# New tables of moves for the second, third and fourth mixer of a four-mixer transformer kernel; the instructions stay the same

## What is computed

```python
def reference(x, ...):
    x = first_block(x, ...)     # layer 0: even_mixer, layer 1: odd_mixer
    return second_block(x, ...) # layer 0: even_mixer_2 + swiglu, layer 1: odd_mixer_2 + swiglu

def odd_mixer(h, w_in, w_out, ...):            # the second mixer, stage "odd"
    proj = h @ w_in
    hq, hf, hi, hg, lx, lg = split_cols(proj, ODD_SIZES)
    hc = rms_norm(hgrn2(hq, hf, hi, lb)) * silu(hg)
    hl = rg_lru(causal_conv(lx, conv_w, conv_b), ...) * silu(lg)
    return concat(hc, hl) @ w_out

# the third mixer, stage "diff": differential attention beside a 31-tap convolution
# the fourth mixer, stage "ssm": latent attention beside a complex state-space scan
```

## Time and profile before

| | us |
|---|---|
| median of 3 runs | 1750.78 (1749.95 to 1752.95) |
| the profiled execution, its own time | 1755.67 |
| its span from first to last instruction | 1753.9 |
| TensorE busy in the span | 1699.9 (97%) |
| VectorE, ScalarE, GpSimd busy | 961.7, 769.7, 949.0 |
| share of the chain that ended last | TensorE 81%, VectorE 11%, ScalarE 4% |

### The profile page before, as it was taken

One profiled execution on the slowest core, in us unless ns is written; L12 is line 12 of the kernel. 1 busy time (PEld: TensorE's weight loads), 2 busy tenths in 40 slices (PEclk: granted clock), 3 DMA queues, 4 the chain that ended last, 5 costly groups with the idle time before them and its releaser, 6 DMA issues.

```text
span 1753.9 us, 21148 instructions
## 1 busy us (share of the span) xinstructions
PE 1699.9 (97%) x7871; PEld 1324.0 (75%) x7871; DVE 961.7 (55%) x1504; ACT 769.7 (44%) x1314; POOL 949.0 (54%) x1108
## 2 busy tenths in 40 slices
PE   9999999998999999899999999999999999999997
PEld 6767668776878776687888888875457888888886
DVE  2033555779966898747614313369786752132344
ACT  4254675477475334754322222354335533222232
POOL 4433224678964463235656656569354565565662
PEclk9999999999999999899999999999999999999998
DMA  5221112222112221022322222221001222222221
GB/s 210 83 84 61 36 49 96 95 73 84 49 37 86 83 85 49 26 83 97 108 97 96 96 96 97 96 72 48 13 24 49 85 96 101 92 97 100 96 96 69
DMA packets 39702, 139.96 MB, mean 80 GB/s; under 512 B 4528, under 2 KB 4656, under 8 KB 39472
## 3 DMA queue, kind: packets, MB, share of 16 engines
q1 hardware_dynamic: 39600, 138.61, 23.4%
HBM read 136.50 MB, written 2.10 MB: 79 GB/s over the span
## 4 chain that ended last, share of the span: by engine, by line
PE 81%; DVE 11%; ACT 4%; issue 2%; POOL 1%; DMA 0%; SPq 0%; DVEq 0%; ACTq 0%
PE ps L889 19%; PE ps L891 18%; PE ps L890 18%; PE ps L910 1%; PE ps L960 1%; PE ps L917 1%; PE ps L962 1%; PE ps L961 1%; DVE ps L1101 1%; PE ps L1178 1%; PE ps L1176 1%; PE ps L1177 1%; PE ps L906 1%; PE ps L1312 1%; PE ps L1636 1%
## 5 line engine op out<-in xcount | busy, mean ns | idle before, releaser
L3165 POOL TENSOR_TENSOR wl<-raw,wh 128x256 fp32r<-128x256 f32 x988 | 801.3, 842 | 710.0 <-ACT wh L1034 704.0
L1034 ACT ACTIVATE wh<-raw 128x1024 fp32r<-128x1024 f32 x246 | 259.4, 1056 | 479.9 <-PE ps L891 441.0
L889 PE MATMUL ps<-hh,wh 128*128 128x512 f32 x1028 | 414.6, 403 | 2.4 <-ACT arena L1472 0.8
L891 PE MATMUL ps<-hh,wl 128*128 128x512 f32 x1028 | 401.3, 390 | 0.0
L890 PE MATMUL ps<-hl,wh 128*128 128x512 f32 x1028 | 401.0, 390 | 0.0
L889 PEld LDWEIGHTS ps<-hh,wh 128*128 128x128 f32 x1028 | 193.5, 188 | 56.2 <-issue 12.0
L890 PEld LDWEIGHTS ps<-hl,wh 128*128 128x128 f32 x1028 | 193.5, 188 | 42.8 <-issue 4.5
L891 PEld LDWEIGHTS ps<-hh,wl 128*128 128x128 f32 x1028 | 193.4, 188 | 41.0
L889 PE MATMUL ps<-mh,wh 128*128 128x512 f32 x540 | 220.0, 407 | 3.4 <-DVE ml L2955 1.4
L891 PE MATMUL ps<-mh,wl 128*128 128x512 f32 x540 | 211.2, 391 | 0.0
L890 PE MATMUL ps<-ml,wh 128*128 128x512 f32 x540 | 210.9, 391 | 0.0
(11 more groups left out here) (497 smaller groups left out, 2746.7 us busy)
## 6 DMA issues: line engine op xcount, KB each, us to landing
raw<-in_w SPq DMA_DIRECT2D x246, 512.0 KB, 3.3
x<-in_x SPq DMA_DIRECT2D x8, 256.0 KB, 8.3
out<-x SPq DMA_DIRECT2D x8, 256.0 KB, 2.0
arena<-in_rope SPq DMA_DIRECT2D x3, 512.0 KB, 4.7
arena<-in_dec SPq DMA_DIRECT2D x1, 1024.0 KB, 6.3
mats<-in_mats SPq DMA_DIRECT2D x1, 576.0 KB, 9.4
raw<-in_w SPq DMA_DIRECT2D x2, 256.0 KB, 3.7
arena<-in_lw SPq DMA_DIRECT2D x1, 512.0 KB, 4.1
```

What stands on the lines that cost most here:

```text
L889: e.matmul(ps[b][:], a, xh, start=first, stop=False)
L891: e.matmul(ps[b][:], l, xh, start=False, stop=final).then_inc(pe.sem, pe.up(*step))
L1034: e.activation(wh[:, n % NHL, :], raw[:, n % NRAW, :], ACT.Copy).then_inc(rounded.sem, rounded.up(n))
L3165: e.tensor_tensor(wl[:, n % NHL, cut(i, 2)], raw[:, n % NRAW, cut(i, 2)], wh[:, n % NHL, cut(i, 2)].bitcast(F32), SUB).then_inc(split.sem, ...
```

## The change

The tables `AHEAD["odd"]`, `AHEAD["diff"]` and `AHEAD["ssm"]` are replaced: 158, 214 and 146 moves become 184, 243 and 164. The table of `even`, the functions that write the first order, the instructions and the order of the weight stream are the same; every engine issues the same instructions in another order. What the new tables were laid out with is an estimate in which a VectorE operation on two tiles in SBUF lasts longer beside a GpSimd operation; that estimate is not in the kernel. In the file the second mixer's table begins so:

```diff
     "odd": [
-        (('w', ('p', 6), 3), ('hn3', 2)), (('hn4', 1), ('w', ('p', 6), 2)), (('hn4', 0), ('hn4', 1)), (('hn3', 1), ('w', ('p', 6),
...
```

## The result

The changed kernel takes **1733.99 us** (median of 4, 1733.88 to 1735.5) against 1751.61 for the kernel before in the same comparison: a ratio of 0.9902, 95% interval 0.9885 to 0.9919. That is 17.2 us less by the ratio and 17.6 by the medians. The forecast was 1743.5 with a range of 1737 to 1754: the direction was right, the gain more than twice the forecast and outside the range. The two profiled executions lie 20.2 us apart (1755.67 and 1735.5), so their stages show some 3 us more than the medians.

The account below looks back on a forecast made before the run. It took TensorE's 34.4 us of idle time in three mixers plus the low clock as the bound, VectorE and GpSimd setting the pace in 380:490. Terms -5.3 + 0 - 2.0 = -7.3 from 1750.8 gave 1743.5 us, range 1737 to 1754.

Parts of the forecast that it names:

- the 0 for the third mixer: Third mixer: new and covered waits taken to leave the stage unchanged, 0 us (-3 to +2.4).
- the -2.0 for the fourth: Fourth mixer: VectorE's two-tile operations run shorter while GpSimd idles; -2.0 us, part of the clock included (-5 to +2.2).
- The second mixer's -5.3: Second mixer: -3.6 us of idle time and -1.7 of low clock, together -5.3.
- The clock term: Low clock: half its cost in 380:490 regained (-1.7), 690:732 unchanged, a part within the fourth mixer's -2.0.
- The opening's wait: Second mixer's opening: TensorE waits at `lm` for VectorE to take out `lx` 3; 0 to 2.7 us, taken as 1.9.
- The level products: Second mixer, head 1's first level product: TensorE waits for GpSimd's product 0 to 3.9 us, taken as 1.5.
- The tail: Second mixer, from `hx` 3 to the first `o` products: a wait of 0 to 7.5 us, taken as 1.0.
- the wait at 715.00: Third mixer: TensorE's longest wait, 2.24 us, read as for GpSimd's last step; stays, less some 1.2 us.
- The gap on GpSimd: Fourth mixer: GpSimd idle some 10 us (1211.7 to 1222), saving VectorE about 4 us ahead of `s4` 0.
- Rival 1: Whole kernel: VectorE and GpSimd are full, no order shortens it, waits only change places; 1749.5 us, chance 0.22.
- Rival 2: Second mixer's tail: the chain keeps its 25.7 us, the first `o` tiles wait 7.5; slower, 1755.3 us, chance 0.18.
- Rival 3: Fourth mixer: two-tile VectorE operations stand still for a whole GpSimd instruction, saving up to 8.9 us; 1738.6 us, chance 0.08.

Follow-up runs that it names:

- e3_ssm: The kernel before with only the fourth mixer's table (`ssm`) replaced by the new one; 1741.66 us, ratio 0.9936 to before.
- e6_late: The changed kernel with the rotation of key 3 put a few operations later on VectorE in the third mixer; 1738.34 us, ratio 0.9915 to before.
- e1_odd: The kernel before with only the second mixer's table (`odd`) replaced by the new one; 1748.42 us, ratio 0.9969 to before.
- e5_fn: The kernel before with `fn` steps 0,2 and 0,3 moved behind the rotation of key 3 on VectorE, third mixer; 1754.22 us, ratio 1.0005.
- e9_r1: The kernel before with six third-mixer moves: `fn` 0,2 and 0,3 behind key 3's rotation, score 11 and its softmax step earlier; 1753.63 us, ratio 1.0005.
- e13_early: The kernel before with `fn` steps 0,2 and 0,3 moved ahead of the rotation of query 3 on VectorE, third mixer; 1748.97 us, ratio 0.9981.
- e4_fill: The changed kernel with angle tables 3 and 4 put back between GpSimd's splits in the fourth mixer, filling its gap; 1737.28 us, ratio 0.9909.
- e7: The kernel before with four of six GpSimd instructions per angle table, from the third table on, cut to a sixteenth of their columns; 1742.22 us, ratio 0.9943.
- e8: The changed kernel with four of six GpSimd instructions per angle table, from the third table on, cut to a sixteenth of their columns; 1732.10 us, ratio 0.9885.
- e10_thin_before: The kernel before with GpSimd's angle tables cut and its weight splits from the second mixer on cut from 256 to 64 columns; 1726.85 us, ratio 0.9852.
- e14_gm: The changed kernel with two GpSimd products (`gm`) moved ahead of a weight slot's split in the second mixer's opening; 1734.76 us, ratio 0.9901.

## Why the prediction was wrong

The steps that failed are two terms of the sum: the 0 for the third mixer, which measured -6.1, and the -2.0 for the fourth, which measured -9.0. The second mixer's -5.3 was near.

**What bounds the kernel.** Right as to the places: 380:490, 690:732 and 1180:1260 are where most of the time came from. Right too that VectorE and GpSimd are near full in the first of them. I then treated VectorE's load as fixed but for one gap. It was not: its operations last longer beside GpSimd's, and the order decides how often.

**The clock term failed in the third and fourth mixer.** I counted 3.3 + 5.0 + 3.2 = 11.5 us for the low clock in the three pieces, missed 1.7 at 1283, and then let 1.7 of it and a part of 2.0 go. By the stretches 1.7, 5.1 and 3.4 us went, 10.2 together. The second mixer's 1.7 was right in this pair of profiles, and by luck: e3_ssm had a full clock there with the old table. I had coupled the clock to no wait in the other two: e6_late shows 0.94 us of idle time more and a mixer 3.2 us longer. In a place where the clock falls, a wait has to be priced with the stretch behind it.

**Second mixer: the sum right (-5.3 forecast, -4.7 measured), the waits in it not.** The opening's wait, taken as 1.9, is 0: VectorE took `lx` 3 out by 342.9 (the first of three outputs that took 1.88 us from 342.28), below the lower end of the 343.2 to 345.9, and TensorE arrived at 343.4. The convolution's blocks took 3.0, 4.1 and 2.9 us, of which I had taken two near the upper end of 4.5. The level products wait 1.59 + 0.78 us, and 0.84 ahead of them for the outputs of `hv`, where I had 1.5. The tail waits 0, where I took 1.0 and kept 7.5 open; the chain from `hx` 3 at 499.02 to the end of the last `hn4` at 517.44 took 18.4 us, where it had taken 25.7. Idle time fell by 1.8 in this pair, where I had 3.6; in the pair with a full clock, e3_ssm and e1_odd, by 3.8. Three sums of mine are off as well, by little: the shift of the opening's output is 8.6 to 11.2 us by its terms, not 8.4 to 11.1; the stage's bounds are -9.7 to +4.4, not -9.4 to +5.3; and in the fourth mixer 3.6 less 1.3 is 2.3, not 2.15.

**Third mixer: the term of 0 failed.** The first score that needs key 3 began at 715.00 and now at 705.77, 9.2 us earlier, 5.0 of them from the mixer's earlier start: the stretch up to there, which I had at +1.0 less 1.2, is 4.2 us shorter. I read the wait at 715.00 as one for GpSimd's last step, and since both scores need the same key, I held it fixed. The chain behind it is ScalarE's, which waited for VectorE's `fn` 0,2. e5_fn and e9_r1, which rested on the same reading, gained nothing, and e13_early, which rested on the other, half of the table's gain. And 3.8 of the 6.1 us are TensorE's busy time, in a piece whose clock I took to stay: the low clock cost 5.1 us before and nothing now.

**Fourth mixer: the mechanism right, its size wrong.** The gap on GpSimd came as forecast, 10.2 us, at 1197 to 1212 and not 1212 to 1222, in a kernel that was 11 us ahead by then. I gave it 4 us on VectorE and less than 2 net; e4_fill prices it at 5.1 on VectorE and 1.3 to 3.0 us of the mixer. But the table spares VectorE 8.4 us in the whole mixer, and e7 and e8 show that without GpSimd's angle work the two orders are level. VectorE's busy time is no price by itself: e8_few_after took 9.4 us more off it, and the mixer got 1.4 us shorter. The scan that took 1205 to 2226 ns, median 1874, in the changed kernel:

```profile
L2927 DVE TENSOR_TENSOR_SCAN hl_scratch<-small,hl_scratch x8: 1193/1213/1683, 1202.3 to 1302.1; 128x512 f32<-128x512 f32 x8
```

**The rivals.** Rival 1 rested on "no order shortens it": 17.2 us of VectorE's busy time say otherwise. Rival 2, the tail, did not come. Rival 3 had the right sign, and the measured time lies 4.6 us below its 1738.6. I argued against whole blocking from the 1245 ns of L2462, taking "0.68 plus a whole split" as what it must show. An instruction that comes in the middle of a split would wait for the rest of it only, so the row did not speak against it. In e10_thin_before, with the splits at a quarter, the same 44 instructions took 681 to 694 ns.

## What to carry to other kernels

When two engines slow each other, their busy time is no fixed load: sum it from the shortest duration of each line, and look at what stands above that as what an order may win back, in part. Count the instructions of each engine in both profiles before calling them the same. When a wait ends at one engine's instruction, look at what the other engines of that place are waiting for in the same microseconds before moving it; a wait that only changes its name was not the chain. And where the clock is low behind a stretch of waits, price the stretch with the waits, as likely, not sure.

## What the runs showed of the hardware

In e14_gm VectorE's operations on 128x4 tiles, which take 0.16 to 0.17 us, took 0.60 to 1.11 us when GpSimd was at a product or a split (up to 350.7 and from 352.6 to 355.5 us):

```profile
349.64 1.11 DVE L1765 TENSOR_TENSOR small<-small 128x4 f32<-128x4 f32 x1
350.79 0.17 DVE L1767 TENSOR_SCALAR small<-small 128x4 f32<-128x4 f32 x1
...
353.43 0.65 DVE L1765 TENSOR_TENSOR small<-small 128x4 f32<-128x4 f32 x1
354.12 0.67 DVE L1767 TENSOR_SCALAR small<-small 128x4 f32<-128x4 f32 x1
354.81 0.65 DVE L1770 TENSOR_TENSOR small<-small 128x4 f32<-128x4 f32 x1
```
```profile
345.63 5.11 POOL L2037 TENSOR_TENSOR arena<-arena 128x512 f32<-128x512 f32 x3
352.60 2.85 POOL L3186 TENSOR_TENSOR wl<-raw,wh 128x256 fp32r<-128x256 f32 x4 [1.86 <-ACT wh L1055]
```

The first ends at 350.75, with GpSimd's product. So the delay is set by GpSimd's instruction and not by VectorE's size: a row of small steps beside long GpSimd instructions pays for it each time. L1767, which reads one tile only, took 0.67 us at 354.12 as well, beside splits.

By the Trainium skill, "SBUF — State Buffer", section "Who interferes with whom", the later of the two engines fully blocks, and an instruction with at most one input in SBUF does not contend outside the 2-port perf modes, which `tensor_scalar` can enter. The row of 1.11 us, which ends with GpSimd's product, agrees with the first. L1767 is a `tensor_scalar`, so its 0.67 us don't speak against the second; no run here shows in which mode it ran. The rule as my prediction gave it, without the modes, is too wide.
